# Shifted value rows prepared during the delta net, and a deeper pipeline in the sliding attention

## The reference

```python
def sink_attention(q, k, v, sinks, key_ok):                       # A
    s = jnp.einsum('bcqkgd,bcskd->bckgqs', q, k) * (HEAD_DIM ** -0.5)
    s = jnp.where(key_ok[None, :, None, None, None, :], s, NEG)
    p = jax.nn.softmax(jnp.concatenate([s, sink], axis=-1), axis=-1)[..., :-1]
    return jnp.einsum('bckgqs,bcskd->bcqkgd', p, v)

def stick_breaking(q, k, v, q_pos, k_pos):                        # B
    z = jnp.einsum('bqhd,bkhd->bhqk', q, k) * (HEAD_DIM ** -0.5)
    visible = k_pos[None, :] < q_pos[:, None]
    log_beta = jax.nn.log_sigmoid(z)
    log_keep = jnp.where(visible, jax.nn.log_sigmoid(-z), 0.0)
    later = lax.cumsum(log_keep, axis=3, reverse=True) - log_keep
    w = jnp.where(visible, jnp.exp(log_beta + later), 0.0)
    return jnp.einsum('bhqk,bkhd->bqhd', w, v)
```

## Time and profile before

| | |
|---|---|
| median of three runs | 1714.48 us |
| the profiled execution | 1717.34 us, its span 1715.7 us |
| granted clock of TensorE, mean | 0.93 |
| PE / PEld busy | 1465.0 us (85%) / 1206.5 us (70%) |
| DVE / ACT / POOL busy | 800.9 / 709.5 / 386.4 us |
| DMA | 177.03 MB, mean 103 GB/s |

### The profile page before, as it was taken

The page is one execution under the profiler, slowest core; times in us unless marked ns, Lnnn a source line. Parts: engine busy times, 40 slices in busy tenths (PEclk is TensorE's granted clock), DMA queues, the critical chain, the costliest instruction groups (busy, mean ns, idle before and its releaser), DMA issues. The chain is left out here.

```text
span 1715.7 us, 31497 instructions
## 1 busy us (share of the span) xinstructions
PE 1465.0 (85%) x12700; PEld 1206.5 (70%) x12700; DVE 800.9 (47%) x1545; ACT 709.5 (41%) x1494; POOL 386.4 (23%) x364
## 2 busy tenths in 40 slices
PE   6999997799999999999995104886799999599996
PEld 5999996789888898888884002554465666477775
DVE  5656676133343333443331202665677787543331
ACT  4567766211221211221110102654466666556563
POOL 0012242123111231122211002553000000145553
PEclk9999998899999999899997656998899999799998
DMA  8554343555243443234433100112200003745551
GB/s 237 174 149 137 122 140 97 147 148 152 76 98 110 121 127 85 73 84 145 116 108 119 63 23 11 50 50 64 80 14 2 14 1 96 201 126 172 169 174 55
DMA packets 201509, 177.03 MB, mean 103 GB/s; under 512 B 30068, under 2 KB 187161, under 8 KB 201369
## 3 DMA queue, kind: packets, MB, share of 16 engines
q1 hardware_dynamic: 154889, 119.73, 23.6%
q0 software_dynamic: 28256, 46.42, 9.8%
q10 hardware_dynamic: 18224, 8.92, 1.9%
HBM read 107.51 MB, written 65.59 MB: 101 GB/s over the span
## 5 line engine op out<-in xcount | busy, mean ns | idle before, releaser
L794 PE MATMUL acc<-side_rows,side_w 128*128 128x384 f32 (+2 forms) x2448 | 459.5, 337 | 5.3 <-ACT side_stage L813 4.2
L794 PEld LDWEIGHTS acc<-side_rows,side_w 128*128 128x128 f32 x2448 | 396.1, 193 | 22.9 <-issue 8.1
L1895 DVE TENSOR_TENSOR_SCAN prod<-keepb,prod 128x512 f32<-128x512 f32 (+4 forms) x184 | 195.6, 1105 | 60.8 <-ACT keepb L1844 59.5
L686 PE MATMUL acc<-side_rows,side_w 128*128 128x384 f32 (+1 forms) x864 | 151.1, 333 | 0.5 <-ACT raw L422 0.5
L686 PEld LDWEIGHTS acc<-side_rows,side_w 128*128 128x128 f32 x864 | 143.9, 191 | 2.8 <-issue 1.2
L1221 DVE COPY base<-b_two 128x256 f32<-128x256 f32 x85 | 36.1, 425 | 219.8 <-PE b_two L1022 219.8
L2008 PE MATMUL b_y<-whi,mhi 128*128 128x512 f32 x272 | 110.0, 404 | 29.3 <-DVE mlo L2061 29.3
L1460 PE MATMUL b_pt<-cf,pr 128*128 128x128 f32 (+2 forms) x280 | 38.6, 282 | 108.9 <-POOL pr L1542 108.9
L813 ACT ACTIVATE side_stage<-acc 128x384 f32<-128x384 f32 (+2 forms) x102 | 46.8, 461 | 195.5 <-PE acc L794 183.9
L1844 ACT ACTIVATE keepb<-b_z 128x1024 f32<-128x1024 f32 (+4 forms) x92 | 82.0, 891 | 109.7 <-PE b_z L1765 67.6
L1460 PEld LDWEIGHTS b_pt<-cf,pr 128*128 128x128 f32 (+2 forms) x280 | 30.1, 143 | 123.1 <-POOL pr L1542 122.4
(11 more groups left out here) (230 smaller groups left out, 2490.1 us busy)
## 6 DMA issues: line engine op xcount, KB each, us to landing
side_rows<-hs_scratch POOLq DMA_DIRECT2D x16, 1536.0 KB, 10.3
hs_scratch<-side_rows SPq DMA_DIRECT2D x34, 512.0 KB, 4.7
mixed<-mix_scratch SPq DMA_DIRECT2D x17, 512.0 KB, 6.7
gates<-sz_scratch SPq DMA_DIRECT2D x17, 512.0 KB, 7.8
side_rows<-hs_scratch POOLq DMA_DIRECT2D x6, 1344.0 KB, 10.2
base<-in_x_prompt SPq DMA_DIRECT2D x15, 512.0 KB
xres<-in_x_prompt SPq DMA_DIRECT2D x15, 512.0 KB
out_y_prompt<-yy POOLq DMA_DIRECT2D x15, 512.0 KB, 6.4
```

Source lines behind the costliest of these rows:

```text
L686: last = pe.matmul(acc[:, u % 2, 0:w], side.w[:, c, w_, k, :], h_[:, b % 2, k, 0:w], start=(k == 0 and p == 0), stop=(k == KT - 1 and p == 2))
L794: last = pe.matmul(self.acc[:, n % 2, 0:width], w[:, w_part, k, :], rows[:, row_part, k, 0:width], start=(k == 0 and i == 0), stop=(k == K ...
L1895: dve.tensor_tensor_scan(prod[0:R, hh, c0:c0 + nk][:, ::-1], kv, kv, prod[0:R, hh, c0 + nk:c0 + nk + 1], ALU.mult, ALU.bypass).then_inc(pr ...
```

## The change

- The copy into `vprev` and the subtracts move into the delta net. The two transfers stand first on SP, ahead of `side.transfers`; POOL does two tiles at the end of each of the passes 4 to 12. `POINTS` loses one piece a pass.
- `vends` and the shifted new rows `dnew` are loaded in the stick breaking from the outputs that already hold the value rows; DVE does the subtract of `dnew`. Two transfers come ahead of `vcprev`, three behind it, and PE waits for all of them.
- In the sliding attention SP loads piece 0 of `uT`, then `sink`, `kc`, `vc`, then the other pieces.
- There, turns run three units behind the scores and products four, and `pr` and the small sums have four buffers.

```diff
@@ delta_net
+                vprev = sb("vprev", [P, TILES, VBW], st=st)
-                POINTS = [8, 6] + [4, 1] * 5 + [4]
+                POINTS = [8, 5] + [4, 1] * 5 + [4]
                     @block.sync
                     def _(sp):
+                        sp.dma_start(vprev[1:P, :, :], vrow[0:P - 1, :, bcols]).then_inc(prev_in, 16)
+                        sp.dma_start(vprev[0:1, 1:TILES, :], vrow[P - 1:P, 0:LAST, bcols]).then_inc(prev_in, 16)
                         side.transfers(sp, begun)
...
+                        def value_differences(tiles_):
+                            for m in tiles_:
+                                if m == 0:
+                                    pool.wait_ge(prev_in, 32)
+                                    pool.wait_ge(first_zero, 1)
+                                pool.tensor_tensor(vrow[:, m, bcols], vprev[:, m, :], vrow[:, m, bcols], ALU.subtract).then_inc(diff_done, 1)
+
+                        pool.memset(vprev[0:1, 0, :], 0.0).then_inc(first_zero, 1)
...
                             for step in steps_done(m, range(7, len(POINTS))):
                                 side.load_rows(pool, step)
+                            if m >= 4:
+                                value_differences(range(2 * (m - 4), min(2 * (m - 3), TILES)))
@@ window_attention
-                pr = sb("pr", [P, 3, AG, 2 * P], st=st)
+                pr = sb("pr", [P, 4, AG, 2 * P], st=st)
-                        for i, n in enumerate(PIECES[:-1]):
-                            rows = slice(n * P, PIECES[i + 1] * P)
+                        def load_piece(i):
+                            rows = slice(PIECES[i] * P, PIECES[i + 1] * P)
                             sp.dma_start(reg[:, 0:5, rows], uT[0:5, :, rows].rearrange("k p t -> p k t")).then_inc(u_in[i], 16)
+
+                        load_piece(0)
+                        sp.dma_start(sink[:, :], io["sinks_a"].to_broadcast([P, AH])).then_inc(sink_in, 16)
                         sp.dma_start(kc[:, :], io["cache_a_k"][0, 0].rearrange("t h d -> t (h d)")).then_inc(cache_in, 16)
                         sp.dma_start(vc[:, :], io["cache_a_v"][0, 0].rearrange("t h d -> t (h d)")).then_inc(cache_in, 16)
-                        sp.dma_start(sink[:, :], io["sinks_a"].to_broadcast([P, AH])).then_inc(sink_in, 16)
-                        sp.dma_start(vprev[1:P, :, :], vrow[0:P - 1, :, bcols]).then_inc(prev_in, 16)
-                        sp.dma_start(vprev[0:1, 1:TILES, :], vrow[P - 1:P, 0:LAST, bcols]).then_inc(prev_in, 16)
-                        sp.dma_start(vends[0:TILES, :], vrow[P - 1:P, :, bcols]).then_inc(prev_in, 16)
-                        sp.dma_start(vends[TILES:TILES + 1, :], vrow[SP0 + NSAMP - 1:SP0 + NSAMP, LAST, bcols]).then_inc(prev_in, 16)
-                        sp.dma_start(dnew[SP0 + 1:SP0 + NSAMP, :], vrow[SP0:SP0 + NSAMP - 1, LAST, bcols]).then_inc(prev_in, 16)
-                        sp.dma_start(dnew[SP0:SP0 + 1, :], io["cache_b_v"][0, 0, PAST - 1:PAST].rearrange("t h d -> t (h d)")).then_inc(prev_in, 16)
+                        for i in range(1, len(PIECES) - 1):
+                            load_piece(i)
@@ window_attention, PE
-                        for n in range(N + 3):
+                        for n in range(N + 4):
                             if n < N:
                                 scores(n)
-                            if 2 <= n < N + 2:
-                                turn(n - 2)
-                            if n >= 3:
-                                values(n - 3)
+                            if 3 <= n < N + 3:
+                                turn(n - 3)
+                            if n >= 4:
+                                values(n - 4)
@@ window_attention, ACT
-                            if n >= 2:
-                                keep(n - 2)
+                            if n >= 3:
+                                keep(n - 3)
                             if n < N:
                                 exps(n)
@@ window_attention, POOL
                         for n, (m, s) in enumerate(units):
-                            if s == 0 and m >= 1:
-                                value_differences(m - 1)
@@ window_attention, DVE
-                            if 2 <= n < N + 2:
-                                keep(n - 2)
+                            if 3 <= n < N + 3:
+                                keep(n - 3)
                             if 1 <= n <= N:
                                 norm(n - 1)
-                            if n >= 4 and n % 2:
-                                keep_out((n - 4) // 2)
+                            if n >= 5 and n % 2 == 0:
+                                keep_out((n - 5) // 2)
@@ stick_breaking
+                        sp.wait_ge(ends_zero, 1)
+                        sp.dma_start(vends[0:LAST, :], prompt[P - PAD - 1:LAST * P - PAD:P, :]).then_inc(ends_in, 16)
+                        sp.dma_start(vends[TILES:TILES + 1, :], sample[NSAMP - 1:NSAMP, :]).then_inc(ends_in, 16)
+                        sp.dma_start(vcprev[1:P, 0, :], old[0:P - 1, :]).then_inc(cache_in, 16)
+                        sp.dma_start(vcprev[:, 1, :], old[P - 1:2 * P - 1, :]).then_inc(cache_in, 16)
+                        sp.dma_start(vnew[new, :], sample).then_inc(cache_in, 16)
+                        sp.dma_start(dnew[SP0:SP0 + 1, :], old[PAST - 1:PAST, :]).then_inc(cache_in, 16)
+                        sp.dma_start(dnew[SP0 + 1:SP0 + NSAMP, :], sample[0:NSAMP - 1, :]).then_inc(cache_in, 16)
...
+                                pe.wait_ge(ends_in, 32)
-                                pe.wait_ge(cache_in, 64)
+                                pe.wait_ge(cache_in, 112)
...
+                        pool.memset(vends[:, :], 0.0).then_inc(ends_zero, 1)
...
+                                dve.tensor_tensor(dnew[new, :], dnew[new, :], vnew[new, :], ALU.subtract).then_inc(vc_done, 1)
```

More of the change, by code:

```diff
@@ L878, in delta_net @@
                 v_ring = sb("v_ring", [P, 2, 2, P], st=st)
+                vprev = sb("vprev", [P, TILES, VBW], st=st)
+                prev_in, diff_done, first_zero = (sem(n, st) for n in ("prev_in", "diff_done", "first_zero"))
                 oss, oln, ors = (sb(n, [P, 4], st=st) for n in ("oss", "oln", "ors"))
@@ L1459, in turn @@
                                 for g in range(AG):
-                                    last = pe.transpose(b_pt[0:kn, t, g, 0:R], pr[0:R, n % 3, g, k0:k0 + kn], ident[0:R, 0:R])
+                                    last = pe.transpose(b_pt[0:kn, t, g, 0:R], pr[0:R, n % 4, g, k0:k0 + kn], ident[0:R, 0:R])
                             last.then_inc(pt_ready, 1)
@@ L1515, in keep @@
                             act.activation(pt[:, n % 2, 0, :, 0:R], b_pt[:, 0, :, 0:R], ACT.Copy).then_inc(pt_kept_act, 1)
-                        for n in range(N + 2):
-                            if n >= 2:
-                                keep(n - 2)
+                        for n in range(N + 3):
+                            if n >= 3:
+                                keep(n - 3)
                             if n < N:
@@ L1624, in stick_breaking @@
                 vcprev = sb("vcprev", [P, 2, VBW], st=st)
+                vends = sb("vends", [32, VBW], st=st)
+                dnew, vnew = (sb(n, [P, VBW], st=st) for n in ("dnew", "vnew"))
                 vend = sb("vend", [P, 2, TILES + 1], st=st)
@@ L1635, in stick_breaking @@
                 names = ("cache_in turned kct_kept z_ready keep_ready one_ready prod_ready wt_ready wt_kept0 wt_kept1 "
-                         "o_ready o_kept part_kept o_stored wo_in vend_ready vend_kept first_zero vc_done").split()
+                         "o_ready o_kept part_kept o_stored wo_in vend_ready vend_kept first_zero vc_done ends_zero ends_in").split()
                 (cache_in, turned, kct_kept, z_ready, keep_ready, one_ready, prod_ready, wt_ready, wt_kept0, wt_kept1,
-                 o_ready, o_kept, part_kept, o_stored, wo_in, vend_ready, vend_kept, first_zero, vc_done) = (sem(n, st) for n in names)
+                 o_ready, o_kept, part_kept, o_stored, wo_in, vend_ready, vend_kept, first_zero, vc_done, ends_zero, ends_in) = (sem(n, st) for n in names)
                 wt_kept = (wt_kept0, wt_kept1)
@@ L1716, in _ @@
                             sp.dma_start(dst[:, :, :], io[name][0, 0].rearrange("(t p) h d -> p t (h d)", p=P)).then_inc(cache_in, 16)
-                        vrows = io["cache_b_v"][0, 0].rearrange("t h d -> t (h d)")
-                        sp.dma_start(vcprev[1:P, 0, :], vrows[0:P - 1, :]).then_inc(cache_in, 16)
-                        sp.dma_start(vcprev[:, 1, :], vrows[P - 1:2 * P - 1, :]).then_inc(cache_in, 16)
+                        old, prompt, sample = (io[n][0, 0].rearrange("t h d -> t (h d)") for n in ("cache_b_v", "p_b_v", "s_b_v"))
+                        sp.wait_ge(ends_zero, 1)
[6 more added lines that the diff above has]
```

(3 more changed lines are left out.)

49 lines of the change are left out of this document (24 added, 25 removed).

## The result

The changed kernel takes **1676.39 us** (median of 4 runs, 1671.62 to 1678.65) where the kernel before takes 1714.46 (1713.56 to 1717.56): a ratio of 0.976, 95% interval 0.973 to 0.979. The profiled execution took 1671.62 us with a span of 1670.0, against 1717.34 and 1715.7.

What follows compares the result with a forecast made beforehand. The delta net was taken as bound by PE, the sliding attention by waits (a copy's hole, a circle of period one). Terms -120 + 88 - 3 + 3 = -32 us off the 1714.48 median gave 1682, range 1662 to 1700.

Steps and rivals of the forecast that it cites:

- POINTS: Delta net, side projection: one piece less in each of 17 passes, 17 more in the last; -3 us, bounds 0 and -6.
- The hole and the pace: Sliding attention: idle stretch gone, earlier first scores, shorter units; -120 us in sum, bounds -103 and -124.
- The head: Sliding attention's start: sink, kc and vc loaded behind the first piece of uT bring unit 2's scores earlier; -12.7 us.
- The pace: Sliding attention: turns three units behind the scores save 0.53 us a turn for 33 turns; -17 us.
- The copy in the delta net: Delta net's start: vprev's copy shuts SP, side_stage's store is late and PE stops; +88 us, bounds +74 and +100.
- give-back: Delta net's last pass: side-projection work moved there costs 6.5 us of the 9.5 moved, gaps taking a part.
- Differences on POOL: Delta net: 17 subtracts on POOL, two a pass, covered by POOL's idle time; 0, without that cover 13 us at most.
- Stick breaking: Stick breaking's start: PE waits longer behind the added vends and new-row transfers; +3 us, bounds 0 and +6.
- That the copy is hidden: Delta net: the second transfer issues at once and PE doesn't stop near 340; 1594 us, chance 0.06.
- That the pace stays: Sliding attention: another circle keeps 4.19 us a unit, so 17 us stay; 1699 us, chance 0.08.
- That ACT's queue is shut as well: Delta net: the first tile's loads on ACT wait too, PE stops at 318 and not 340; 1693 us, chance 0.08.
- The slower case: Delta net: the copy shares its engine throughout; at 89 ns a row the stop grows by 87, 1769 us; chance 0.06.

Runs made afterwards that it cites:

- the first experiment: The changed kernel with only its 127-partition copy into vprev cut into 112 and 15 partitions: 1585.28 us, 0.924 of before.

## Why the prediction came out

The forecast was 1682 in 1662 to 1700, measured 1676.39. Each mechanism that the sum named was there, but that it came so near is in part luck. In the two profiled executions the terms are -125.3, +93.6, -13.9 and +2.0, which makes -43.6 and not -32: the 5.3 too little that the attention was given and the 5.6 too little that the copy was charged cancel, and the 10.9 that `POINTS` was short stay. The medians show -38.1, and so the miss is 6.

- **The hole and the pace**: -120 with bounds -103 and -124; measured -125.3, a little past the end. The head gave 13.4 (predicted 12.7; 12.6 by its own experiment), the unit 3.64 us (3.71), the waits before turns went to 1.2 us in all. The pace was put at 17 and is 19.5 of waits and some 2 of clock at the end: the sum left out that PE, once it doesn't wait there, also keeps its clock through the last units.
- **The copy in the delta net**: +88 with bounds 74 and 100; measured some +93.6 (79.7 plus the 13.9 by which the delta net of `POINTS` 6 is longer, 714.6 against 700.7). The stop began at 337 and not 340, and ended at 429.88 and not 425.5. SP was shut for 106.98 us (90 to 110 had been named). What was short is the copy. Its first rows moved between 311.5 and 312.0, some 2.5 us after its issue, where 1.6 was taken. SP is not shut to its end: 2,043 of its 2,159 rows had moved by queue q1 when the issue behind it was over (2,043 or 2,044 in the four other kernels with this copy and this order too). The last 116 take 5.3 us more at 45.9 ns, so the copy was over at about 422.3, an estimate, where the sum has 418.8, or 417.2 for a stage that begins 1.6 us earlier. The store of unit 8, issued at 420.11, landed at 429.0, 6.7 behind that; the sum gave 5.7. Sharing was taken at 10 us and cost some 13 (106.98 less 2,043 rows at 45.9 ns, the copy's start included; an estimate), of which POOL's rows are 8.8. One reading under this term was too neat: that the issue of 96.61 us in before equals the 96.5 worked out for the copy is chance. There other loads kept the DMA share at 1.01 or more until 948, five us into that issue, and about one engine (0.07) was busy until 1047, seven us beyond its end. Nor is SP shut for nearly the whole of a small copy: 127 rows would take 5.7 us at 44.7 ns, and the issue behind them took 2.15.
- **POINTS**: -3 with bounds 0 and -6; measured -13.9. This is the term that was mis-sized. The give-back of 6.5 came out as 6.5, and the pieces moved saved some 9.5, as counted (8.3 in the passes other than 5 and 11, and a piece of 0.56 in each of these two). What was missed is the clock: before has a stretch of PE at 1.2 GHz in pass 11, which goes with one piece less; the pass is 9.3 us shorter, 8.7 more than its piece. Another 2.1 beyond the piece lie in pass 5, of which 1.5 can't be put down to `POINTS`, since five of the seven kernels with 5 pieces lack them. In the long stretch of the earlier trace rows the slow one was thinned to a mean clock of 0.98, and the sum priced every matmul there at its mean. Three shorter stretches of before show it (busy us and count of PE, PEld, DVE, ACT, POOL; clock, DMA share, GB/s):
```profile
345.00:700.00 355.00, 351.54 (x4101) 313.03 (x4100) 129.35 (x389) 72.36 (x192) 73.79 (x102) 1.00 0.40 111
700.00:740.00 40.00, 36.55 (x429) 31.99 (x428) 18.06 (x43) 11.35 (x28) 6.48 (x9) 0.79 0.27 74
740.00:920.00 180.00, 178.75 (x2122) 159.98 (x2122) 63.09 (x201) 32.70 (x92) 37.98 (x52) 1.00 0.39 112
```
- **Differences on POOL**: 0, and 0 it is: apart from the 4.4 at the stage's start, which before has too, no wait of PE in the delta net for POOL is longer than the 2.56 at its end (4.07 before).
- **Stick breaking**: +3, measured +2.0. The wait forecast as 11 is 2.85 for `vends` and 7.79 for `dnew`.
- **The rivals.** That the copy is hidden fell: SP was shut for 106.98 us. The rule of the Trainium skill that spoke for it ("DMA: Bandwidth & Descriptors", Rules for kernel authors: issue early, wait late) does describe the kernel of the first experiment, where the copy is cut, lands 17 us after its issue and stops nobody; it does not describe the uncut copy, behind which SP can issue nothing. The same table of the Trainium skill says that two transfers to disjoint halves of the partitions are not worth it; here two parts, of 112 and 15, save 91 us, for the one transfer of 127 partitions kept only about one engine of sixteen busy (DMA share 0.07). That the pace stays fell with the unit of 3.64. That ACT's queue is shut as well fell: while SP was shut, ACT issued loads of a tile at 323.01 and 323.41 in 0.37 and 0.53 us, and PE ran on to 337. The slower case, sharing throughout, fell with some 13 us in all: alone, from 337 to 415 us, the copy moved 1,700 rows in 78 us, 45.9 ns a row (44.7 in before).

## What to carry to other kernels

A transfer that runs on one engine cost about the same in both places here; moving it chose who waits, and everything behind it on its issuing queue waited with it. So mend its shape before its place: the cut at 112 partitions was worth 85 us in the old place and 91 in the new, while moving the uncut copy gained nothing (90 us of hole gone from the attention, 125.3 less the head's 13.4 and the 21.8 of the pace; 93.6 come in the delta net). The 38 us of the change come from its other parts: put back one at a time, the third unit of distance, the order of the loads and the piece cost 22.5, 14.2 and 13.3 us, more than 38 together.

And where PE is the bound, look at the granted clock of every pass before you price its work by a mean: 575 us at a mean of 0.98 held 17 us at half clock, which went with one piece of work less in the pass; what ties the two is not shown.

## What the runs showed of the hardware

- A copy of 127 partitions and 2,159 rows of 1 KB ran at 44.7 to 45.9 ns a row, on about one engine of sixteen, and what SP issued next took 96.61 to 106.98 us (109.33 for two weight loads together). Cut into 112 and 15 partitions its parts landed 14.3 and 16.6 us after their issues, and the issues behind the first took 3.80, 2.25 and 6.03 us (8.52 and 1.25 in the attention).
- What is shut is the queue of the issuing engine: ACT's transfers went in 0.37 and 0.53 us meanwhile. SP is shut until nearly all of the copy has moved: 2,043 or 2,044 of 2,159 rows in the five kernels in which the edge rows stand behind the uncut copy in the delta net.
- POOL's loads of rows, at the same time, cost the issue behind the copy 8.8 us (106.98 to 98.15).
- After 92 us of standstill PE ran at a granted clock of 0.50 from 429 to 433 us and at 0.99 from 433 to 440, while in the delta net, where PE is busy 566.84 of 575 us, it ran at 1.2 GHz for 17.1 us behind two waits of 1.78 and 1.46 us, and for 6.8 us behind the same first wait in another kernel with the same code there. What sets the length no run here shows.
